# The second block's keys, receptances and values as seven half-size products, in a stage of their own behind the gates' plain tile

## The chip, the cores and the metric

The kernel runs on one core of a Trainium2 chip. The metric is the device time of one execution in microseconds (us); lower is better. One core has a matrix engine (TensorE, PE in the rows), a vector engine (VectorE, DVE), a scalar engine (ScalarE, ACT), GpSimd (POOL) and a sync engine (SyncE, SP) that issues the weight transfers. Each runs its own instruction list in order; semaphores make one wait for another.

## The reference

Three transformer blocks run one after the other on 512 tokens of width 1024, in float32. The change is in the second block, where 16 meta tokens come in front (528 tokens). What matters of it:

```python
def centred_shift(p, mu):
    prev = jnp.pad(p[:, :-1], ((0, 0), (1, 0), (0, 0)))
    nxt = jnp.pad(p[:, 1:], ((0, 0), (0, 1), (0, 0)))
    return p + mu[0] * (prev - p) + mu[1] * (nxt - p)
...
    u = rms_norm(h, mix_norm_g[i])
    proj = u @ w_in[i]
    p_rwkv, p_q, p_k, p_v, p_gate_a, p_gate_b = jnp.split(proj, IN_SPLITS, axis=-1)
...
    z = centred_shift(p, shift_mu)
    r, k, v, wd, ad, gd = jnp.split(z, RWKV_SPLITS, axis=-1)
```

So the first 1952 columns of the projection, 512 each for receptances (r), keys (k) and values (v) and 416 for the low-rank inputs of decay, in-context rate and gate, are products of the normed activations, and each is then mixed with its neighbours in time: own part times (1 - mu0 - mu1), plus mu0 times the token before, plus mu1 times the token behind. The keys are also scaled by `k_k` and normed per head of 64. From these a two-directional recurrence over the 528 tokens starts.

## The kernel before

**Layout.** Activations stand with channels on the 128 partitions and the 528 tokens along the free dimension, in slabs of eight 128-channel chunks. `H` is the normed input, `X` the residual, `S2` to `S6` work slabs. Weights come in tiles of 1024 x 512 through a ring of slots (SyncE, `issue_weights`).

**The stage (lines 2365 to 2369).** One `DenseStage` computes four weight tiles: `rwkv_gates` (chunks 12 to 15, the last of 32 channels), `rwkv_k` (4 to 7), `rwkv_r` (0 to 3), `rwkv_v` (8 to 11). Its unit is one chunk by one half of the tokens (264): eight accumulating matmuls (line 393), then a ScalarE copy out of PSUM into `raw` (`keep_raw`, line 2287). After the second half of a chunk VectorE mixes it (`shift`): own part (2282), token before (2283), token behind (2285). There are 32 units; four PSUM banks go round.

**What sets the order.** Each engine's list is written out by `woven`: after every unit each *lane* may put one step of side work. Lane one, from unit 1: `FirstNorm` (827), the norm of the first block's end, eight steps on VectorE. Lane two, from unit 10: `Gates` (on ScalarE a tanh and two sigmoids at 2248 to 2250, then eight small products 2241 and 2242 with a ScalarE copy 2255 each), then `unit_keys`, a `HeadNorm` of the keys (squares 923 on ScalarE, sums 888 and 896 on TensorE, root on ScalarE, floor and reciprocal 955 and 959 on VectorE, then four times a spread 911 on TensorE and a scaling 964 on VectorE). Lane three, from unit 16: `Factors` of the recurrence's first piece (products 3104 and 3114 on TensorE, ScalarE 3120 to 3155, VectorE 3182 to 3231). Ahead of the first unit stand the block's norms (`TwoNorms`).

**Stage ends.** A stage is a block: all engines meet at its end before any begins the next. After this one comes `recurrence` (first matmuls at line 3344).

**Seven products.** `SevenProducts` (2516) exists already and is used by other matrices here. It takes two chunks (a pair) and both token halves as a 2 x 2 block product and needs seven products of four matmuls where plain units need 32 matmuls. Per pair, VectorE makes sums of weights ("third", "second", "first", "fourth", each 128x512, lines 2714, 2746, 2749, 2767) and puts the seven banks together with seven 128x264 additions (2758 to 2778); ScalarE copies two banks (2688, 2692). Products go in the order 4, 1, 6, 7, 2, 5, 3: product 6 waits for "second", product 3 for "fourth". A lane step stands behind product 1, 7, 5 and 3: four steps per pair. In a `SevenStage` VectorE's lanes are one step behind those of the other engines (`later`). `post` is what is done with a finished pair; with `by="dve"` VectorE does it in the next pair's first step, behind that pair's "second" and "first", or, at the end of a matrix, before anything of the next matrix (`finish`). Before, no pair of the recurrence's inputs goes this way.

## Time and profile before

| | us |
|---|---|
| median of 3 runs | 3779.97 (3779.03 to 3781.15) |
| span of the profiled execution | 3776.2 |
| TensorE busy | 3490.8 (92% of the span) |
| VectorE busy | 1319.4 (35%) |
| ScalarE busy | 665.2 (18%) |
| first unit of the stage to the first matmul of the recurrence | 1659.63 to 1807.46 |

The profiled span is 3.8 us below the median of the runs; what lies around the span is not in the profile. Times in the rows count from the span's start. A timeline row gives a group of like instructions: start, time to the end of the last, engine, line, what it writes and reads, and in brackets the idle time before it and who ended it. One matmul on float32 shows as two records, so "x16" there is eight matmuls.

### The profile page before, as it was taken

The numbers are of one execution on the slowest core, as the hardware profiler recorded it, in microseconds if no ns is written. First come the engines' busy times: TensorE is split into PE (matmuls) and PEld (weight loads), VectorE is DVE, ScalarE is ACT, GpSimd is POOL, SyncE is SP. The second block draws the span as 40 slices with busy tenths as digits, with TensorE's granted clock in tenths as the row PEclk, the third lists the DMA queues.
The fourth block names the chain that finished last, engine by engine and source line by source line (L and its number), as shares of the span: only waits on it lengthen the run. The fifth ranks groups of instructions, "written<-read, shape, count | busy, mean of one in ns | idle before, by whom it ended". The sixth has DMA issues, their size and how long they took to land. (4 is left out here: it accounts for less than half of the span.)

```text
span 3776.2 us, 56173 instructions
## 1 busy us (share of the span) xinstructions
PE 3490.8 (92%) x24676; PEld 2304.4 (61%) x24676; DVE 1319.4 (35%) x2796; ACT 665.2 (18%) x1461; POOL 78.3 (2%) x128
## 2 busy tenths in 40 slices
PE   8999999798988889889888899999999999999997
PEld 4444678433332333257667777778888855887666
DVE  1211456310111101133666344345533623544344
ACT  2111540200000000013343114112100001101231
POOL 0000000000000000000222000000000000000000
PEclk9999999999999999999999899999999999999999
DMA  6233101799999999950000210222222111221110
GB/s 252 103 132 112 45 24 49 315 428 427 428 428 425 423 427 427 426 214 1 3 4 4 85 56 23 79 82 88 68 90 90 67 67 54 81 89 34 53 62 23
DMA packets 125842, 593.73 MB, mean 157 GB/s; under 512 B 7296, under 2 KB 37632, under 8 KB 99232
## 3 DMA queue, kind: packets, MB, share of 16 engines
q1 hardware_dynamic: 125600, 590.14, 39.2%
q8 instruction: 196, 3.21, 0.4%
q14 instruction: 46, 0.38, 0.0%
HBM read 588.02 MB, written 2.10 MB: 156 GB/s over the span
## 5 line engine op out<-in xcount | busy, mean ns | idle before, releaser
L2656 PE MATMUL banks<-slabs,ring 128*128 128x256 f32 (+1 forms) x3472 | 770.4, 382 | 0.2 <-DVE ring L2767 0.2
L2656 PEld LDWEIGHTS banks<-slabs,ring 128*128 128x128 f32 x3472 | 657.3, 190 | 103.6 <-issue 7.6
L1991 PE MATMUL banks<-ring,slabs 128*64 128x512 f32 x2304 | 520.2, 599 | 80.6 <-DMA ring<-in_w_exp 69.3
L393 PE MATMUL banks<-slabs,ring 128*128 128x264 f32 (+3 forms) x1736 | 568.5, 485 | 6.0 <-PEq L323 2.5
L393 PEld LDWEIGHTS banks<-slabs,ring 128*128 128x128 f32 (+1 forms) x1736 | 326.9, 191 | 222.2 <-issue 186.6
L1991 PEld LDWEIGHTS banks<-ring,slabs 128*64 128x64 f32 x2304 | 163.4, 137 | 413.1 <-issue 318.7
L2128 DVE TENSOR_TENSOR work<-work,banks 128x512 f32<-128x512 f32 x32 | 22.0, 687 | 487.3 <-PE banks L1991 487.3
L1991 PE MATMUL banks<-slabs 128*64 128x512 f32 x768 | 171.9, 596 | 21.4 <-DMA slabs<-in_w_exp 18.5
L2861 PE MATMUL banks<-slabs,ring 128*128 128x264 f32 x768 | 172.4, 386 | 1.6 <-issue 1.6
L2861 PEld LDWEIGHTS banks<-slabs,ring 128*128 128x128 f32 x768 | 145.8, 190 | 26.8 <-issue 1.9
L393 PE MATMUL banks<-ring,slabs 128*128 128x512 f32 (+3 forms) x560 | 158.6, 439 | 0.8 <-PEq L323 0.8
L2636 PE MATMUL banks<-slabs,ring 128*128 128x256 f32 (+1 forms) x576 | 135.4, 395 | 9.4 <-PEq L323 7.5
L1991 PEld LDWEIGHTS banks<-slabs 128*64 128x64 f32 x768 | 54.4, 137 | 132.2 <-issue 107.6
L393 PEld LDWEIGHTS banks<-ring,slabs 128*128 128x128 f32 (+1 forms) x560 | 91.2, 188 | 70.3 <-issue 67.5
L2636 PEld LDWEIGHTS banks<-slabs,ring 128*128 128x128 f32 x576 | 111.4, 196 | 32.1 <-issue 13.1
L2072 ACT ACTIVATE work<-banks 128x512 f32<-128x512 f32 x32 | 19.1, 597 | 542.7 <-PE banks L1991 542.7
L2135 DVE COPY slabs<-banks 64x512 f32<-64x512 f32 x32 | 22.0, 689 | 261.2 <-PE banks L1991 261.0
L1297 ACT ACTIVATE slabs<-slabs,small 128x513 f32<-128x513 f32 (+7 forms) x136 | 97.1, 714 | 88.3 <-DVE small L1253 88.2
L2746 DVE TENSOR_TENSOR ring<-ring 128x512 f32<-128x512 f32 (+1 forms) x65 | 46.6, 717 | 174.9 <-PE banks L2656 171.6
L1168 PE MATMUL banks<-slabs 64*128 64x256 f32 (+10 forms) x544 | 97.3, 438 | 8.8 <-DVE small L1249 4.5
L2688 ACT COPY slabs<-banks 128x256 f32<-128x256 f32 (+1 forms) x51 | 19.2, 376 | 402.0 <-PE banks L2656 402.0
L2656 PE MATMUL banks<-ring 128*128 128x256 f32 (+1 forms) x336 | 78.8, 384 | 0.0
(544 smaller groups left out, 3841.7 us busy)
## 6 DMA issues: line engine op xcount, KB each, us to landing
ring<-in_w_exp SPq DMA_DIRECT2D x144, 2048.0 KB, 15.8
slabs<-in_w_exp SPq DMA_DIRECT2D x48, 2048.0 KB, 31.8
ring<-in_w_in SPq DMA_DIRECT2D x19, 2048.0 KB, 10.9
ring<-in_w_ff SPq DMA_DIRECT2D x16, 2048.0 KB, 8.2
ring<-in_even_w_in SPq DMA_DIRECT2D x14, 2048.0 KB, 8.0
ring<-in_w_ada SPq DMA_DIRECT2D x12, 2048.0 KB, 8.1
ring<-in_w_out SPq DMA_DIRECT2D x4, 2048.0 KB, 8.2
ring<-in_even_w_out SPq DMA_DIRECT2D x4, 2048.0 KB, 7.8
```

The source lines that it names most:

```text
L393: mm = core.nc.tensor.matmul(to, lhsT, rhs, start=kk0 + k < g, stop=kk0 + k >= kcs - g)
L1168: mm = nc.tensor.matmul(score[h][0:m, at:at + cols], *products[j], start=j == 0, stop=j == count - 1)
L1297: nc.scalar.activation(r, r, ACT.Exp, bias=st[0:m, h:h + 1], scale=scale, accum_out=st[0:m, 2 + h:3 + h]).then_inc(e_ready.sem, e_ready.ad ...
L1991: ins = mm(out[64 * c:64 * c + CAP, :], lhsT[:, k, :], w[:, at:at + 512], start=first and k == 0, stop=last and k == 3)
L2072: nc.scalar.activation(sg, G[:, :], ACT.Silu).then_inc(moe["silu"].sem, moe["silu"].add(1))
L2128: nc.vector.tensor_tensor(hid, sg, U[:, :], ALU.mult).then_inc(moe["hidden"].sem, moe["hidden"].add(1))
L2135: ins = nc.vector.tensor_copy(y[64 * s:64 * s + CAP, 512 * half:512 * half + 512], Y[64 * half:64 * half + CAP, :])
L2636: last = mm(self.bank["plain", at], A[i][k // h][:, k % h, :], self.B[k // h][j][:, k % h, :], start=k == 0, stop=k == 2 * h - 1)
L2656: last = mm(self.bank[p, which], a[:, k, :], b[:, k, :], start=k == 0, stop=k == h - 1)
L2688: self.done(nc.scalar.copy(self.to(p, 1, 0), self.bank[p, 4]), "held")
L2746: self.done(tt(A[1][1], A[1][1], A[1][0], ALU.subtract), "second")
L2861: last = mm(self.bank(which), a[:, k, :], self.fourth(t, k) if which == 4 else b[:, k, :], start=t == 0 and k == 0, stop=t == 1 and k == 7)
```

## The change

The stage is cut in two. A `DenseStage` keeps the gates' tile alone, with `FirstNorm` beside it and a new side, `HalfSums`, which makes the four sums of `H` (128x1056 each) into `S3`. A `SevenStage` behind it computes keys, receptances and values as two pairs each by `SevenProducts`, without a plain first pair, all three on the same sums and the same small scratch; `Gates` and `unit_keys` run in its lane from step 0, `Factors` from step 10 of 24. The mixing's own part becomes a ScalarE activation with a scale per partition (`own_part`, two of 128x528 per pair), done before the next pair's first copy; the two neighbour parts stay on VectorE (`neighbours`, four instructions per pair) as `post`. A pair's second set of two scratch buffers goes. Semaphores are shared out anew so that the stage has the counts it needs.

```diff
--- before
+++ after
-    raw, z = [S2, S3], [S4, S5]
+    raw, z, four = S2, [S4, S5], 4
...
-        p_, z_ = raw[ch // KC][rows, ch % KC, :], z[ch // KC][rows, ch % KC, :]
+        p_, z_ = raw[rows, ch % KC, :], z[ch // KC][rows, ch % KC, :]
         step(nc.vector.tensor_scalar(z_, p_, own[rows, ch:ch + 1], None, ALU.mult))
...
-    keep_raw = lambda eng, ps, ch, t0, t1: nc.scalar.copy(raw[ch // KC][0:ps.shape[0], ch % KC, t0:t1], ps)
+    keep_raw = lambda eng, ps, ch, t0, t1: nc.scalar.copy(raw[0:ps.shape[0], ch % KC, t0:t1], ps)
+    raw_of = lambda at, p: raw[:, at + 2 * p:at + 2 * p + 2, :]
+
+    def own_part(at, first):
+
+        def scaled(act, p):
+            for i in range(2):
+                ch = first + 2 * p + i
+                ins = nc.scalar.activation(z[ch // KC][:, ch % KC, :], raw_of(at, p)[:, i, :], ACT.Copy, scale=own[:, ch:ch + 1])
+            return ins
+        return scaled
+
+    def neighbours(at, first):
+
+        def post(dve, p):
+            step = Chain(dve, shifted)
+            for i in range(2):
+                ch = first + 2 * p + i
+                p_, z_ = raw_of(at, p)[:, i, :], z[ch // KC][:, ch % KC, :]
+                step(nc.vector.scalar_tensor_tensor(out=z_[:, 1:T], in0=p_[:, 0:T - 1], scalar=core.col("mu0", ch), in1=z_[:, 1:T], op0=ALU.mult, op1=ALU.add))
+                ins = nc.vector.scalar_tensor_tensor(out=z_[:, 0:T - 1], in0=p_[:, 1:T], scalar=core.col("mu1", ch), in1=z_[:, 0:T - 1],
+                                                     op0=ALU.mult, op1=ALU.add)
+            return ins
+        return post
...
-    def gates_shifted(act):
-
-        act.wait_ge(shifted.sem, shifted.at(3 * 4))
-    gates = Gates(core, 1, S5, gw, g, T, gates_shifted)
-    gates_pe = gates.pe
-
-    def after_loads(pe):
-
-        pe.wait_ge(core.loaded.sem, core.loaded.at(16 * len(loads)))
-        yield from gates_pe(pe)
-    gates.pe = after_loads
+    gates = Gates(core, 1, S5, gw, g, T, lambda act: None)
     first = FirstNorm(norms, lambda k: core.col("final", k))
     unit_keys = HeadNorm(core, 2, S4[:, 4:8], 4, T, S6[:, 4:8], core.rstd[:, :], core.c("common", "halves32"), core.c("common", "pick8"), 2, 1, 0.0,
                          lambda c: gains[:, 16 + c:17 + c], S6[:, 4:8], (6, 5, 6), core.work[:, 2 * RW + 2 * WIDE:2 * RW + 2 * WIDE + 50],
-                         first=lambda act, c: act.wait_ge(shifted.sem, shifted.at(3 * (5 + c))), scale=lambda c: core.col("k_k", c), floor=1e-12)
...
     def after_gates(pe):
 
         pe.wait_ge(gates.s["chunk"].sem, gates.s["chunk"].at(8))
-        pe.wait_ge(first.s["shifted"].sem, first.s["shifted"].at(1))
         yield from keys_pe(pe)
     unit_keys.pe = after_gates
+
+    in_halves = lambda k, a, b: H[:, 4 * k:4 * k + 4, a:b]
+    def products(name, at, first, places):
+        return SevenProducts(core, name, in_halves, T, core.slab[3], places, lambda p: raw_of(at, p), neighbours(at, first), "dve", plain=False,
+                             sums_of=name, scaled=own_part(at, first))
+    places = spare[:, :, :].rearrange("p k c -> p (k c)")[:, 4 * WIDE:]
+    some = lambda: Carve(places)
+    keys, receptances, values = products("rwkv_k", 0, 4, some()), products("rwkv_r", 4, 0, some()), products("rwkv_v", 0, 8, some())
+    values.place_free = lambda engine, p: keys.pair_done(engine, p)
+    sums_of_h = HalfSums(keys, core.rwkv["step"], lambda dve: dve.wait_ge(norms.s["chunk"].sem, norms.s["chunk"].at(KC)))
...
         if what == "keys":
-            chunk(8)
+            keys.pair_done(engine, 0)
+            receptances.pair_done(engine, 0)
         if what == "unit_keys":
...
-            chunk(12)
+            values.pair_done(engine, 0)
...
-    DenseStage(core, [("rwkv_gates", units_of(of_h, T, keep_raw, post=("dve", shift), first=12)),
-                      ("rwkv_k", units_of(of_h, T, keep_raw, post=("dve", shift), first=4)),
-                      ("rwkv_r", units_of(of_h, T, keep_raw, post=("dve", shift))),
-                      ("rwkv_v", units_of(of_h, T, keep_raw, post=("dve", shift), first=8))],
-               banks=range(4), before=[norms], loads=loads, lanes=[(1, [first]), (10, [gates, unit_keys]), (16, [ahead_of_tiles])], pool_too=True).run()
+    DenseStage(core, [("rwkv_gates", units_of(of_h, T, keep_raw, post=("dve", shift), first=12))], banks=range(4), before=[norms], loads=loads,
+               lanes=[(1, [first]), (3, [sums_of_h])]).run()
+    SevenStage(core, [keys, receptances, values], banks=range(4), lanes=[(0, [gates, unit_keys]), (10, [ahead_of_tiles])], pool_too=True).run()
...
         else:
             self.after(engine, "out12", p - self.plain + 1)
+        if self.scaled:
+            self.after(engine, "scaled", p - self.plain + 1)
         self.done(self.post(engine, p), "rows")
...
             nth = p - self.plain + 1
+            if self.scaled and nth > 1:
+                self.after(act, "out12", nth - 1)
+                self.done(self.scaled(act, p - 1), "scaled")
             self.product_done(act, p, 4)
             self.place_free(act, p)
...
+        if self.scaled:
+            self.after(act, "out12", self.count - self.plain)
+            self.done(self.scaled(act, self.count - 1), "scaled")
...
-            s1, u2, u3 = self.s1[p % 2], self.u2[p % 2], self.u3[p % 2]
+            s1, u2, u3 = self.s1[p % 2], self.u2, self.u3
...
+class HalfSums(Side):
+
+
+    def __init__(self, products, count, ready):
+        self.products, self.count, self.inputs_ready = products, count, ready
+
+    def pe(self, pe):
+        yield
+
+    act = pe
+
+    def dve(self, dve):
+        tt, step = self.products.core.nc.vector.tensor_tensor, Chain(dve, self.count)
+        B, (T1, T2, T3, T4) = self.products.B, self.products.T
+        self.inputs_ready(dve)
+        tt(T3, B[1][1], B[0][1], ALU.subtract)
+        step(tt(T1, B[0][1], B[0][0], ALU.subtract))
+        yield
+        step(tt(T2, B[1][1], T1, ALU.subtract))
+        yield
+        tt(T4, B[1][0], T2, ALU.subtract)
+        yield
```

Line numbers of the changed kernel differ: matmuls of the seven products stand at 2653, gates' products at 2240 and 2241, unit keys' at 887, 895 and 910, `Factors`' at 3173 and 3183; on VectorE the neighbour parts at 2305 and 2306, "third", "second", "first" at 2759, 2791, 2794, the last addition of a pair at 2823, `HeadNorm` at 954, 958 and 963, `Factors` from 3251 to 3300.

The first place is VectorE's list around the reciprocals of the unit keys. Before, from the mixing of one chunk on:

```order
L2282 TENSOR_SCALAR slabs<-slabs,small 128x528
L2283 SCALAR_TENSOR_TENSOR slabs<-slabs,param 128x527
L2285 SCALAR_TENSOR_TENSOR slabs<-slabs,param 128x527
L955 TENSOR_SCALAR work<-work 128x32
L955 TENSOR_SCALAR work<-work 16x8
L959 RECIPROCAL work<-work 128x32
L959 RECIPROCAL work<-work 16x8
L964 SCALAR_TENSOR_TENSOR slabs<-slabs,gains,banks 128x528
```

Now, from "second" of the second pair of receptances on:

```order
L2791 TENSOR_TENSOR ring<-ring 128x4x128
L2794 TENSOR_TENSOR ring<-ring 128x4x128
L2305 SCALAR_TENSOR_TENSOR slabs<-slabs,param 128x527
L2306 SCALAR_TENSOR_TENSOR slabs<-slabs,param 128x527
L2305 SCALAR_TENSOR_TENSOR slabs<-slabs,param 128x527
L2306 SCALAR_TENSOR_TENSOR slabs<-slabs,param 128x527
L954 TENSOR_SCALAR work<-work 128x32
L954 TENSOR_SCALAR work<-work 16x8
L958 RECIPROCAL work<-work 128x32
L958 RECIPROCAL work<-work 16x8
L963 SCALAR_TENSOR_TENSOR slabs<-slabs,gains,banks 128x528
```

Between the mixing's three instructions and the reciprocals (955, 959) there was nothing else; now "second", "first" (which needs the pair's product 1) and the four neighbour parts of the pair before stand ahead of them (954, 958).

The second place is TensorE's list there. Before:

```order
L393 MATMUL banks<-slabs,ring 128x264 x8
L3104 MATMUL banks<-slabs,work 128x264
L393 MATMUL banks<-slabs,ring 128x264 x8
L911 MATMUL banks<-common,work 64x128 x8
L911 MATMUL banks<-common,work 64x16 x2
L3104 MATMUL banks<-slabs,work 128x264
```

Now:

```order
L2653 MATMUL banks<-slabs,ring 128x264 x4
L3173 MATMUL banks<-slabs,work 128x264
L2653 MATMUL banks<-slabs,ring 128x264 x8
L910 MATMUL banks<-common,work 64x128 x8
L910 MATMUL banks<-common,work 64x16 x2
L3173 MATMUL banks<-slabs,work 128x264
```

The spread of the first chunk (911 before, 910 now), which reads the reciprocals, stands behind the pair's products 4 and 1, and products 6 and 7 behind it.

The third place is the end of VectorE's list in the stage. Before:

```order
L3222 TENSOR_TENSOR slabs<-slabs 128x528
L3223 SCALAR_TENSOR_TENSOR slabs<-slabs,param 128x528
L2282 TENSOR_SCALAR slabs<-slabs,small 128x528
L2283 SCALAR_TENSOR_TENSOR slabs<-slabs,param 128x527
L2285 SCALAR_TENSOR_TENSOR slabs<-slabs,param 128x527
L3231 SCALAR_TENSOR_TENSOR slabs<-banks,ring 128x264 x2
L2282 TENSOR_SCALAR slabs<-slabs,small 128x528
L2283 SCALAR_TENSOR_TENSOR slabs<-slabs,param 128x527
L2285 SCALAR_TENSOR_TENSOR slabs<-slabs,param 128x527
```

Now:

```order
L2816 TENSOR_TENSOR slabs<-banks,ring 128x264
L3288 TENSOR_TENSOR ring<-ring,slabs 128x2x528
L3289 TENSOR_TENSOR ring<-ring,work 128x2x528
L2823 TENSOR_TENSOR slabs<-banks,ring 128x264
L3291 TENSOR_TENSOR slabs<-slabs 128x528
L3292 SCALAR_TENSOR_TENSOR slabs<-slabs,param 128x528
L2305 SCALAR_TENSOR_TENSOR slabs<-slabs,param 128x527
L2306 SCALAR_TENSOR_TENSOR slabs<-slabs,param 128x527
L2305 SCALAR_TENSOR_TENSOR slabs<-slabs,param 128x527
L2306 SCALAR_TENSOR_TENSOR slabs<-slabs,param 128x527
L3300 SCALAR_TENSOR_TENSOR slabs<-banks,ring 128x264 x2
```

The last chunk's mixing, three instructions, was the end, with the recurrence's bonus (3231) ahead of it; now two chunks' neighbour parts stand behind the last addition (2823) and two of `Factors`, and the bonus (3300) behind them.

## Rows read from the trace of the kernel before

**Rows 1.** The page: span, and TensorE busy over it (share, instructions).

```profile
span 3776.2 us, 56173 instructions
...
PE 3490.8 (92%) x24676; PEld 2304.4 (61%) x24676; DVE 1319.4 (35%) x2796; ACT 665.2 (18%) x1461; POOL 78.3 (2%) x128
```

**Rows 2.** Windows of 20 us: busy (count) by engine; PEclk; DMA share, GB/s.

```profile
1680.00:1700.00 20.00, 20.00 (x90) 14.09 (x89) 9.05 (x13) 1.87 (x5) 0.00 (x0) 1.00 0.30 105
...
1780.00:1800.00 20.00, 20.00 (x106) 16.79 (x105) 15.47 (x20) 4.48 (x8) 0.00 (x0) 1.00 0.00 1
```

**Rows 3.** Timeline of TensorE: start, us, line, [idle before <-releaser].

```profile
1656.06 3.78 PE L764 MATMUL banks<-common,small 128*128 128x128 f32 x16
...
1659.63 44.33 PE L393 MATMUL banks<-slabs,ring 128*128 128x264 f32 x192
...
1705.31 0.71 PE L2241 MATMUL banks<-slabs,ring 128*128 128x264 f32 x2 [1.34 <-ACT slabs L2250]
...
1706.59 3.83 PE L393 MATMUL banks<-slabs,ring 128*128 128x264 f32 x16
...
1747.40 2.88 PE L888 MATMUL banks<-slabs,common 128*32 128x512 f32 x16 [1.19 <-ACT slabs L923]
...
1764.33 1.31 PE L911 MATMUL banks<-common,work 128*64 128x128 f32 x20
...
1807.46 1.16 PE L3344 MATMUL banks<-ring 64*64 64x64 f32 x64 [3.09 <-PEq L323]
```

**Rows 4.** Groups by line and shape, 1650 to 1810: count, busy, mean ns, idle before.

```profile
L2283 DVE SCALAR_TENSOR_TENSOR slabs<-slabs,param 128x527 f32<-128x527 f32 x15 | 11.5, 768 | 0.5
...
L2282 DVE TENSOR_SCALAR slabs<-slabs,small 128x528 f32<-128x528 f32 x15 | 7.3, 488 | 57.5 <-ACT slabs L2287 57.5
```

**Rows 5.** Timeline of VectorE, same columns, in and after the stage.

```profile
1691.28 0.75 DVE L2285 SCALAR_TENSOR_TENSOR slabs<-slabs,param 32x527 f32<-32x527 f32 x1
...
1762.66 0.24 DVE L955 TENSOR_SCALAR work<-work 128x32 f32<-128x32 f32 x2
...
1762.93 0.40 DVE L959 RECIPROCAL work<-work 128x32 f32<-128x32 f32 x2
...
1787.53 1.26 DVE L3216 TENSOR_TENSOR ring<-ring,slabs 128x1056 f32<-128x1056 f32 x1
...
1800.92 0.43 DVE L3231 SCALAR_TENSOR_TENSOR slabs<-banks,ring 128x264 f32<-128x264 f32 x1 [1.55 <-PE banks L3114]
...
1806.15 0.77 DVE L2285 SCALAR_TENSOR_TENSOR slabs<-slabs,param 128x527 f32<-128x527 f32 x1
```

**Rows 6.** Timeline of ScalarE: four 128x528 activations.

```profile
1746.52 2.61 ACT L923 ACTIVATE slabs<-slabs,param 128x528 f32<-128x528 f32 x4
```

**Rows 7.** Timeline of TensorE in the seven-product stage of wo2, and its end.

```profile
2459.27 37.54 PE L2656 MATMUL banks<-slabs,ring 128*128 128x264 f32 x168
...
2499.99 2.04 PE L572 MATMUL banks<-slabs,common 128*32 128x512 f32 x32 [3.17 <-PEq L323]
```

**Rows 8.** Timeline of VectorE in that stage, one pair of chunks.

```profile
2475.49 0.69 DVE L2749 TENSOR_TENSOR ring<-ring 128x512 f32<-128x512 f32 x1 [1.09 <-PE banks L2656]
...
2479.05 0.43 DVE L2761 TENSOR_TENSOR slabs<-banks,slabs 128x264 f32<-128x264 f32 x1 [1.35 <-PE banks L2656]
```

**Rows 9.** Windows of 1 us: TensorE busy and PEclk, its granted clock.

```profile
712.00:713.00 1.00, 1.00 (x7) 1.00 (x7) 0.00 (x0) 0.00 (x0) 0.00 (x0) 0.59 1.04 442
...
1654.00:1655.00 1.00, 0.46 (x5) 0.38 (x4) 0.56 (x4) 0.24 (x2) 0.00 (x0) 0.95 0.00 0
...
1661.00:1662.00 1.00, 1.00 (x4) 0.82 (x3) 1.00 (x3) 0.00 (x0) 0.00 (x0) 0.64 0.00 0
...
1808.00:1809.00 1.00, 1.00 (x44) 0.93 (x37) 0.30 (x2) 0.70 (x1) 1.00 (x2) 0.75 0.00 0
...
2500.00:2501.00 1.00, 1.00 (x20) 0.45 (x24) 0.00 (x0) 0.00 (x0) 0.00 (x0) 1.00 1.04 375
```

**Rows 10.** Timeline of TensorE after a long idle time in the first block.

```profile
709.62 5.35 PE L1960 MATMUL banks<-area,slabs 128*128 128x128 f32 x32 [1.56 <-DVE area L2110]
```

64 lines of the change are left out of this document (40 added, 24 removed).

## The prediction

> **What bounds the kernel now.** I read first the page's busy shares, then windows of 20 us over the stage, then the three engines' timelines in it. The page gives TensorE 92% of the 3776.2 us span [rows 1]; in the stage it is 20.00 of 20 us busy in nearly every window, at clock 1.00, while VectorE is at 9.05 where only mixing runs and at 15.47 in the last full window, where `Factors` has joined in [rows 2]. So TensorE bounds the stage, with two small stalls of 1.34 us (the gates' product waiting for tanh and sigmoid) and 1.19 us (unit keys' sums waiting for squares) [rows 3]. Behind the last unit TensorE is idle 3.09 us until the recurrence's first matmul at 1807.46 [rows 3]: the last chunk is still mixed, the last instruction starting at 1806.15 and lasting 0.77 [rows 5], so the next stage starts 0.54 us after VectorE's end. The reader is to see two things: what is saved on TensorE counts in full, as long as TensorE stays the bound; and the stage's end is set by VectorE.
>
> **What TensorE saves.** 192 records take 44.33 us and two records are one matmul, so a matmul of 264 columns is 0.46 us with the slow start, and less without: the wo2 stage, seven products at the same size, does 84 in 37.54 us without a pause, 0.445 each [rows 3, 7]. Keys, receptances and values were 24 units of 8, 192 matmuls. Now they are six pairs of 28, 168 matmuls. 24 x 0.445 = **10.7 us saved**. The wait of 1.19 us goes too, since the gates' and keys' work lies differently: squares are ready before the sums are reached. The gates' wait for tanh and sigmoid, 1.34 us, stays, since their chain still starts behind the second copy and TensorE has as much to do as before until the first small product; I take +0.2. The lanes' TensorE work is the same, but the two bonus products, with their switching 1.2 us, move behind the stage's last product and are counted there. Sum: -10.7 - 1.2 + 0.2 - 1.2 = **-12.9 us**.
>
> **The new stage border.** The 192 records are 12 units in 44.33 us, so the gates' eight units end 29.6 us behind 1659.63, near 1689.4 with the last drain [rows 3]. VectorE still mixes that chunk of 32 channels, its last part ending at 1692.03 [rows 5], and then has two steps of `FirstNorm` left, 0.75 each (this kind of instruction takes 0.768 on 527 columns, and these are 512 [rows 4]), to 1693.5. All engines meet, 0.54 us as at the recurrence's start. TensorE starts again at 1694.0: **+4.6 us** in which before it had work. `HalfSums` (four of 128x1056 at 1.26 [rows 5]) lies under the units of the gates, in which VectorE has over half its time free; I cost it at nothing.
>
> **The work on VectorE.** Own parts go: 12 x 0.488 = 5.9 us [rows 4]. Weight sums and additions come: per pair four at 0.69 and seven at 0.43 [rows 8], 5.8 us, for six pairs 35. That is cheap where VectorE waits anyway; where it does not, its order decides. I walked the three lists step by step with the rows' durations: 0.80 us from an instruction to one that depends on it and 0.68 to one that does not for the neighbour parts (so a pair's four take 3.0), and 0.20 from a product's end to its reader. TensorE's stalls in that walk:
>
> - Keys to receptances. The last keys pair is put together 0.65 after its last product; ScalarE (behind a gates' copy) makes the own parts, 2 x 0.65 [rows 6]; VectorE mixes, 3.0, and only then makes "third" and "second" of the receptances, 1.4. TensorE meanwhile has products 4 and 1 and two gates' products, 6.1 us, and waits **1.1**.
> - The unit keys' reciprocals. Before, floor and reciprocal ran at 1762.66, and the spread at 1764.33 found them done [rows 3, 5]. Now they stand behind "first", which needs product 1 of the same pair, and behind four neighbour parts; TensorE meets the spread right after product 1. That is 0.2 + 0.6 + 3.0 + 0.7 (955 and 959 together [rows 5]), less the little that overlaps: **4.4**.
> - Receptances to values: like the first, with a `HeadNorm` scaling and a scan of 1.36 before it, **1.8**.
> - The last pair. From "first" on VectorE never pauses: 0.6, mixing 3.0, two of `Factors` 1.4, three additions 1.3, a 128x1056 and a 128x528 of `Factors` 2.0; only then "fourth", 0.7, for which product 3 waits: **2.0**.
>
> Together **+9.3 us**, no row of which the trace of before shows. Then the end: behind product 3 stand VectorE's two 128x1056 (2.3, partly under it), the last addition, two of `Factors` 1.5 (ScalarE's own parts lie under them), the last two chunks' mixing 3.0, a bonus 0.43, the second bonus product, which TensorE may only start when the first bank is read (one matmul 0.45 and two handovers, 0.8), a bonus 0.43 [rows 5], and 0.54 to the next stage. From product 3's end to the recurrence I get 8.4 us, before it was 3.3: **+5.1 us**.
>
> Sum at full clock: -12.9 + 4.6 + 9.3 + 5.1 = **+6.1 us**. The part of it that is a sum of rows in a fixed order (border, end) I hold to within 1 us; the four stalls hang on the walk, 9.3 with an error of 3 either way.
>
> **The clock.** Rows show TensorE's granted clock at either 1.00 or 0.50, which is 2.4 and 1.2 GHz. Behind the 3.09 us of idleness and small 64-column work at 1807.46 it fell (0.75 is the mean of the microsecond in which it did); at 2500, after an idle 3.17 us, it was still 1.00 [rows 3, 7, 9]. The new border (4.6 us) and the wait for the reciprocals (4.4) are longer than any gap in this stage, so no row decides whether dense work behind them starts slow. When it was low and dense work came, it rose late: 709.62 to about 712.8 and, with a low start at 1656.06, about 1661.7 [rows 3, 9, 10], that is 3.2 to 5.7 us at half rate. It costs half of that, 1.6 to 2.8 us; I take 2.2 for each of the two gaps, and 0.6 for the recurrence's first matmuls (1.16 us), which so far began at full clock. The bounds are 0 and 6.2. I take the low clock at both, since the idle time is half as long again as the one at 2500 that just held. Together **+5.0 us**. On this the Trainium skill ("TensorE: Matmul & The Clock Gate", section "Why this matters for your kernels") has a rule that speaks against the change: no idle gaps between bursts of matmuls in mid kernel, since idleness brings the half clock back. By it both gaps pay and the sum stays at +11; by the row at 2500 alone neither pays and it is +6.
>
> The Trainium skill ("Perfetto Trace Analysis", section "Optimizing Scalar/DVE Operations") also says that moving work to ScalarE pays where VectorE is saturated. In the windows here VectorE is not saturated before [rows 2]; at the new end it is, but there the moved part is hidden on ScalarE, and the order, not the load, makes the wait.
>
> **Forecast.** +6.1 + 5.0 = +11.1 us on the profiled execution's 3776.2, which stands 3.8 below the median. On the median that is 3780.0 + 11.1 = **3791.1 us**.
>
> **Rivals.**
> - *The clock holds.* Same stalls, no low clock: +6.1, **3786.1**. For it speaks 2500, against it the length of the gaps.
> - *The order is kinder than I walked it: not slower.* If ScalarE and VectorE finish each pair early enough that TensorE never waits at the four places, only border and end remain: -12.9 + 4.6 + 5.1 = -3.2, **3776.8**, and with the stalls half as long 3781. It decides at the reciprocals: if they are done within products 6 and 7's time. VectorE's load over the stage is only some 75 us of 119 (35 of sums and additions, 24 x 0.768 = 18 of neighbour parts [rows 4], some 20 of `Factors` and unit keys), which speaks for it; the lists as they now stand speak against it.
> - *VectorE falls further behind.* The end is a chain of some 19 us on one engine; if each dependent step costs 0.1 us more than the rows (scratch in one buffer, not two), or ScalarE's own parts come behind `Factors`' activations, stalls grow by 5 and the clock falls once more: +17, **3797**.
> - *The own part does not leave the path.* ScalarE's two activations stand between the last addition and the mixing, 1.3 us plus two handovers, where before VectorE took 1.0. Where nothing hides it (both changes of matrix) it adds 0.7 each; that is in the 1.1 and 1.8 already and no case of its own.
>
> **Chances.** Forecast with low clock at one or both gaps 0.60 (3787.5 to 3794), clock holds 0.17, kinder order 0.12, further behind 0.11. The range takes the forecast, the clock's rival and half of each outer one (0.6 + 0.17 + 0.11): 3782 to 3797, the bounds of the walk's error on either side of it. Over 0.2%, 7.6 us, is about what a measurement of this kernel can tell from no change: slower, from 3787.5 up, is 0.58 of the forecast's case, 0.04 of the clock's and 0.10 of the last, together 0.72; same is 0.25; faster, below 3772.4, needs the kinder order and some gain that I have no term for, 0.03.
>
> **What would show it.** In the changed profile: 24 fewer matmuls in the stage; TensorE idle about 4.6 us between the gates' tile and the first product; a wait of about 4.4 us of the first spread of the unit keys (910) for the reciprocals (958); waits of 1 to 2 us of products for "second" at receptances' and values' first pairs and for "fourth" in the last; 8 us from the last product to the recurrence's first matmul, only bonus products in it; and half clock for 3 to 6 us behind the first two. I am wrong if the spread finds its reciprocals ready, if the clock stays at 1.00, or if time moves in the recurrence, which has the same instructions as before.

## The result and the profile after

| | before | after |
|---|---|---|
| device time, median of 4 runs | 3779.5 us (3778.5 to 3781.2) | 3793.8 us (3792.9 to 3796.0) |
| profiled execution's span | 3776.2 us | 3792.3 us |
| mean granted TensorE clock | 0.982 | 0.977 |
| gates' first unit to the recurrence's first matmul | 147.83 us | 161.70 us |
| of it, TensorE busy | 142.21 us | 141.24 us |
| of it, TensorE idle | 5.62 us | 20.46 us |
| mean granted clock in it | 0.99 | 0.90 |

After over before is 1.0038, with a 95% interval of 1.0024 to 1.0053: slower, by 14 us. The page of the changed kernel, beside [rows 1]:

```profile
span 3792.3 us, 56192 instructions
...
PE 3492.1 (92%) x24628; PEld 2306.6 (61%) x24628; DVE 1350.1 (36%) x2854; ACT 669.3 (18%) x1461; POOL 77.7 (2%) x128
```

The stretch that the change touches is measured from the gates' first unit to the recurrence's first matmul [rows 3]; I call it the stretch from here on. Its whole-window row in the changed kernel (busy time and count of PE, PEld, DVE, ACT, POOL; granted clock; DMA share; GB/s):

```profile
1659.49:1821.19 161.70, 141.24 (x623) 104.69 (x623) 91.13 (x152) 39.06 (x71) 0.40 (x4) 0.90 0.04 14
```

It is 13.9 us longer than before, of the 16.1 by which the two profiles differ. The recurrence behind it is as long as it was: 304.20 us from its first matmul to the next stage's, before 304.32. The rest of the kernel, span less stretch, is 3628.4 us before and 3630.6 after, and in the runs below it scatters between 3623 and 3632 without a cause in the code. So here the stretch is the ruler, and the device time only confirms its sign. The stretch has a scatter of its own, since each kernel has one profile: the first four products behind the border took 9.04, 9.89, 10.06 and 10.41 us in four kernels whose lists are the same up to there. I therefore read a difference between two stretches row by row, and take one of under 3 us, my estimate from such rows, as no difference by itself.

TensorE's timeline in the changed kernel (start, us, engine and line, operands, count, [idle before it <- what ended the idle]). L392 is the gates' plain tile, L2653 the seven products, L910 the unit keys' spread, L3183 the two bonus products, L3413 the recurrence. This answers to [rows 3]:

```profile
1659.49 29.90 PE L392 MATMUL banks<-slabs,ring 128*128 128x264 f32 x128
1693.65 9.89 PE L2653 MATMUL banks<-slabs,ring 128*128 128x264 f32 x32 [4.26 <-PEq L322]
1704.87 0.71 PE L2240 MATMUL banks<-slabs,ring 128*128 128x264 f32 x2 [1.34 <-ACT slabs L2249]
...
1738.07 3.80 PE L2653 MATMUL banks<-slabs,ring 128*128 128x264 f32 x16 [1.53 <-DVE ring L2791]
1741.80 1.11 PE L887 MATMUL banks<-slabs,common 128*32 128x512 f32 x16
...
1758.95 2.30 PE L910 MATMUL banks<-common,work 128*64 128x128 f32 x20 [4.34 <-DVE work L958]
1761.19 1.25 PE L3173 MATMUL banks<-slabs,work 64*128 64x264 f32 x2
1762.36 6.12 PE L2653 MATMUL banks<-slabs,ring 128*128 128x264 f32 x16
...
1786.35 5.49 PE L2653 MATMUL banks<-slabs,ring 128*128 128x264 f32 x16 [2.10 <-DVE ring L2791]
...
1810.63 3.10 PE L2653 MATMUL banks<-slabs,ring 128*128 128x264 f32 x8 [1.94 <-DVE ring L2812]
1815.68 1.25 PE L3183 MATMUL banks<-slabs,common 128*128 128x264 f32 x2 [1.95 <-DVE slabs L3292]
1819.15 1.25 PE L3183 MATMUL banks<-slabs,common 128*128 128x264 f32 x2 [2.23 <-DVE slabs L3300]
1821.19 1.99 PE L3413 MATMUL banks<-ring 64*64 64x64 f32 x64 [0.79 <-PEq L322]
```

VectorE's rows at the two longest of these waits: the last steps of `FirstNorm` (L826) ahead of the border, and "first" (L2794), the last of the four neighbour parts (L2306) and the reciprocals (L958) ahead of the spread:

```profile
1691.92 1.41 DVE L826 SCALAR_TENSOR_TENSOR slabs<-slabs,param,banks 128x512 f32<-128x512 f32 x2
...
1754.65 0.69 DVE L2794 TENSOR_TENSOR ring<-ring 128x512 f32<-128x512 f32 x1 [1.03 <-PE banks L2653]
...
1757.54 0.77 DVE L2306 SCALAR_TENSOR_TENSOR slabs<-slabs,param 128x527 f32<-128x527 f32 x1
...
1758.50 0.40 DVE L958 RECIPROCAL work<-work 128x32 f32<-128x32 f32 x2
```

The times in brackets in TensorE's timeline add up to the 20.5 us of idleness: 4.26 at the border, 1.34 for tanh and sigmoid, 1.53 and 2.10 for "second" (L2791) at the receptances' and the values' first pairs, 4.34 for the reciprocals (L958), 1.94 for "fourth" (L2812) and 1.95, 2.23 and 0.79 at the end. Before they were three rows, 1.34, 1.19 and 3.09 [rows 3]. So 14.8 us of idle time came. And the busy time hardly fell, though 24 matmuls are gone. The groups by line show why (count; busy us, mean ns; idle before):

```profile
L2653 PE MATMUL banks<-slabs,ring 128*128 128x264 f32 x336 | 87.3, 418 | 9.8 <-PEq L322 4.3 <-DVE ring L2791 3.6 <-DVE ring L2812 1.9
L392 PE MATMUL banks<-slabs,ring 128*128 128x264 f32 (+1 forms) x128 | 29.9, 395 | 0.0
```

L392 and L2653 together take 117.2 us; before, the 512 records of the same kind took 119.9 in this stretch. The 418 ns of L2653 against 395 of L392 are its slow parts: the group of 32 at 1693.65 takes 9.89 us, where the same group takes 7.36 at full clock (in a run below), and a group of 16 takes 3.83 at full clock, but 6.12 at 1762.36 and 5.49 at 1786.35. One-microsecond windows of the changed kernel behind the border, in the wait for the reciprocals, behind the wait of 2.10 us, and in product 3 of the last pair; before, the windows of the stretch that [rows 2] shows read 1.00:

```profile
1692.00:1693.00 1.00, 0.00 (x0) 0.00 (x0) 1.00 (x2) 0.00 (x0) 0.00 (x0) 0.50 1.06 412
1757.00:1758.00 1.00, 0.00 (x0) 0.00 (x0) 0.96 (x2) 0.00 (x0) 0.00 (x0) 0.50 0.00 0
1788.00:1789.00 1.00, 1.00 (x4) 0.80 (x3) 0.00 (x0) 0.00 (x0) 0.00 (x0) 0.50 0.00 0
1812.00:1813.00 1.00, 1.00 (x3) 0.77 (x3) 1.00 (x2) 0.00 (x0) 0.00 (x0) 0.50 0.00 0
```

The low clock's cost from the rows:

| where | at low clock | at full clock | lost |
|---|---|---|---|
| first four products | 9.89 | 7.36 | 2.5 |
| spread, a lane's product, group of 16 behind it | 2.30 + 1.25 + 6.12 | 1.31 + 0.71 + 3.83 | 3.8 |
| group of 16 behind the 2.10 us | 5.49 | 3.83 | 1.7 |
| product 3 of the last pair | 3.10 | 2.05 | 1.0, hidden under VectorE |
| the two bonus products | 2 x 1.25 | 2 x 0.71 | 1.1, the first hidden |

That is 10.1 us of busy time, of which some 8.5 lengthen the stretch. It eats up most of the 10.2 us of busy time that the 24 matmuls had given (119.9 less 109.7, which is 117.2 at full clock).

### The profile page after: what moved, and what is told of

It reads as the page before. It is cut to its first block and busy times, and to the rows that moved or that the text cites. A ratio compares the mean times of both kernels' runs of the same rounds, so it can differ in the third digit from the quotient of the medians.

```text
span 3792.3 us, 56192 instructions
## 1 busy us (share of the span) xinstructions
PE 3492.1 (92%) x24628; PEld 2306.6 (61%) x24628; DVE 1350.1 (36%) x2854; ACT 669.3 (18%) x1461; POOL 77.7 (2%) x128
## 5 line engine op out<-in xcount | busy, mean ns | idle before, releaser
L2653 PE MATMUL banks<-slabs,ring 128*128 128x256 f32 (+1 forms) x3808 | 857.7, 385 | 10.1 <-PEq L322 4.3
L2653 PEld LDWEIGHTS banks<-slabs,ring 128*128 128x128 f32 x3808 | 724.6, 191 | 132.1 <-issue 24.2
L392 PE MATMUL banks<-slabs,ring 128*128 128x512 f32 (+3 forms) x1352 | 477.5, 511 | 6.0 <-PEq L322 2.5
L392 PEld LDWEIGHTS banks<-slabs,ring 128*128 128x128 f32 (+1 forms) x1352 | 254.6, 191 | 205.4 <-issue 181.4
L2930 PEld LDWEIGHTS banks<-slabs,ring 128*128 128x128 f32 x768 | 145.8, 190 | 26.8 <-issue 1.9
L392 PE MATMUL banks<-ring,slabs 128*128 128x512 f32 (+3 forms) x560 | 158.6, 439 | 0.8 <-PEq L322 0.8
L2674 PE MATMUL banks<-slabs,ring 128*128 128x256 f32 (+1 forms) x576 | 135.9, 398 | 9.4 <-PEq L322 7.5
L392 PEld LDWEIGHTS banks<-ring,slabs 128*128 128x128 f32 (+1 forms) x560 | 91.2, 188 | 70.3 <-issue 67.5
L2674 PEld LDWEIGHTS banks<-slabs,ring 128*128 128x128 f32 x576 | 113.6, 199 | 30.4 <-issue 12.8
L2791 DVE TENSOR_TENSOR ring<-ring 128x512 f32<-128x512 f32 (+1 forms) x71 | 50.8, 715 | 183.8 <-PE banks L2653 178.9
L2730 ACT COPY slabs<-banks 128x264 f32<-128x264 f32 (+1 forms) x57 | 21.5, 377 | 410.7 <-PE banks L2653 410.7
L2653 PE MATMUL banks<-ring 128*128 128x256 f32 (+1 forms) x336 | 78.7, 384 | 0.0
## 6 DMA issues: line engine op xcount, KB each, us to landing
ring<-in_w_in SPq DMA_DIRECT2D x19, 2048.0 KB, 11.1
```

The lines of the kernel that those rows point to most:

```text
L392: mm = core.nc.tensor.matmul(to, lhsT, rhs, start=kk0 + k < g, stop=kk0 + k >= kcs - g)
L2653: last = mm(bank, a[:, k, :], b[:, k, :], start=k == 0, stop=k == h - 1)
L2674: last = mm(self.bank["plain", at], A[i][k // h][:, k % h, :], self.B[k // h][j][:, k % h, :], start=k == 0, stop=k == 2 * h - 1)
L2730: self.done(nc.scalar.copy(self.to(p, 1, 0), self.bank[p, 4]), "held")
L2791: self.done(tt(A[1][1], A[1][1], A[1][0], ALU.subtract), "second")
L2930: last = mm(self.bank(which), a[:, k, :], self.fourth(t, k) if which == 4 else b[:, k, :], start=t == 0 and k == 0, stop=t == 1 and k == 7)
```

## The experiments

Each kernel is a small edit away from a neighbour. The four of the first group ran on one chip beside the kernel before (median 3777.5 us there), the next three on one with it at 3779.9, the last with it at 3778.7. Ratios are to the kernel before of the same group.

| kernel | stretch | time, ratio [95%] |
|---|---|---|
| before | 147.8 | 1 |
| after | 161.7 | 1.0038 [1.0024, 1.0053] |
| the border alone (e1_split_plain) | 153.8 | 1.0019 [1.0009, 1.0028] |
| after, reciprocals sooner (e2_lane_before_mixing) | 154.3 | 1.0017 [1.0007, 1.0026] |
| after, fillers in two waits (e3_filler) | 155.5 | 1.0026 [1.0017, 1.0035] |
| after, own part on VectorE (e4_own_on_vector) | 166.1 | 1.0039 [1.0025, 1.0054] |
| after, one stage (e5_one_stage) | 147.4 | 0.9990 [0.9981, 0.9999] |
| e5 and two orders (e6_one_stage_orders) | 145.5 | 0.9994 [0.9985, 1.0003] |
| after and the two orders (e7_two_stages_orders) | 151.3 | 0.9999 [0.9990, 1.0008] |
| e6, later idle turn out, end reordered (e8_end_order) | 142.9 | 0.9982 [0.9973, 0.9991] |

**The border alone.** The kernel before with its stage cut in two behind the gates; keys, receptances and values stay plain units, mixing as before.

```diff
-    DenseStage(core, [("rwkv_gates", units_of(of_h, T, keep_raw, post=("dve", shift), first=12)),
-                      ("rwkv_k", units_of(of_h, T, keep_raw, post=("dve", shift), first=4)),
...
+    DenseStage(core, [("rwkv_gates", units_of(of_h, T, keep_raw, post=("dve", shift), first=12))], banks=range(4), before=[norms], loads=loads, lanes=[(1, [first])]).run()
+    DenseStage(core, [("rwkv_k", units_of(of_h, T, keep_raw, post=("dve", shift), first=4)),
...
-               banks=range(4), before=[norms], loads=loads, lanes=[(1, [first]), (10, [gates, unit_keys]), (16, [ahead_of_tiles])], pool_too=True).run()
+               banks=range(4), lanes=[(2, [gates, unit_keys]), (8, [ahead_of_tiles])], pool_too=True).run()
```

> The kernel before with its stage cut in two and nothing else: the gates' tile with FirstNorm in one stage, keys, receptances and values as 24 plain units in the next, Gates and unit keys from its unit 2, Factors from its unit 8 (places they had before). It prices the new border by itself. My theory (a border is idle time plus a low clock behind it): TensorE idle about 4.3 us behind the gates' tile, half clock for 3 to 5 us behind that, so the recurrence's first matmul 6 to 7 us later than before and the time 3785 to 3787. Rival (the border is only the idle time; what the changed kernel lost beyond it is the seven products' own): 4.3 us, 3783 to 3784, clock at 1.00.

TensorE's timeline, the border and the end:

```profile
1692.16 16.16 PE L393 MATMUL banks<-slabs,ring 128*128 128x264 f32 x64 [4.26 <-PEq L323]
...
1811.82 1.98 PE L3335 MATMUL banks<-ring 64*64 64x64 f32 x64 [3.09 <-PEq L323]
```

The stretch is 153.82 us, 6.0 longer: 4.26 idle, the same figure as in the changed kernel, and 1.7 of low clock in the group behind it (16.16 us, where 64 such records take 14.51 at full clock). The end's 3.09 is that of before. A border costs 6 to 7 us here, whether plain units follow it (4.26 + 1.7) or seven products (4.26 + 2.5). This kernel has no `HalfSums`, and its border is no shorter: the sums of `H` cost nothing, as forecast.

**The reciprocals sooner.** VectorE takes its turn for the unit keys ahead of the four neighbour parts of the pair before, not behind them. Nothing else changes.

```diff
-            if self.post and self.by == "dve" and p:
+            if self.post and self.by == "dve" and p and not self.scaled:
                 self.finish(dve, p - 1)
...
             yield
+            if self.post and self.by == "dve" and p and self.scaled:
+                self.finish(dve, p - 1)
```

> The changed kernel with one edit: a pair's neighbour parts come behind VectorE's lane step of the next pair's first step, not ahead of it, so the unit keys' floor and reciprocal stand right behind first. My theory (the 4.34 us wait for the reciprocals is the four neighbour parts ahead of them, and the 3.8 us of half-clock work behind it is that wait's doing): the wait falls to 1.3 to 1.6 us, the clock stays at 1.00 there, the time falls by 5 to 7 us to 3787 to 3789. Rival (it is VectorE's load, not its order: what is moved comes back behind): the wait goes to product 3 or the next second, the time stays within 2 us of the changed kernel's 3793.8.

```profile
1738.12 3.80 PE L2653 MATMUL banks<-slabs,ring 128*128 128x264 f32 x16 [1.53 <-DVE ring L2791]
...
1756.04 1.31 PE L910 MATMUL banks<-common,work 128*64 128x128 f32 x20 [1.38 <-DVE work L958]
...
1779.62 5.49 PE L2653 MATMUL banks<-slabs,ring 128*128 128x264 f32 x16 [2.10 <-DVE ring L2791]
...
1803.90 3.27 PE L2653 MATMUL banks<-slabs,ring 128*128 128x264 f32 x8 [1.94 <-DVE ring L2814]
```

The spread now waits 1.38 us and runs in 1.31, at full clock; the stretch is 154.26 us, 7.4 shorter. By the rows, 3.0 of this is the wait (1.38 for 4.34) and 3.8 the low clock behind it. Another 0.9 is a shorter low clock behind the border (9.04 for 9.89), which the edit doesn't reach, and the end is 0.2 longer. The products' waits are the changed kernel's to the hundredth (1.53, 2.10, 1.94), and the group behind the 2.10 again takes 5.49, so the rival, by which the wait comes back further on, is refuted. The reciprocals' place thus cost 6.8 us: of the wait of 4.34, forecast as 4.4, the neighbour parts were 3.0, and the clock was 3.8 against the 2.2 of the prediction.

**Fillers.** The changed kernel with 8 and 9 matmuls whose result nobody reads, put where TensorE would wait at the border and for the reciprocals. VectorE's and ScalarE's lists stay as they are, so only the clock can gain.

```diff
-                lanes=[(1, [first]), (3, [sums_of_h])]).run()
+                lanes=[(1, [first]), (3, [sums_of_h]), (7, [Filler(core, H, core.bank[4], 8)])]).run()
...
+    unit_keys.filler = Filler(core, H, core.bank[5], 9)
```

> The changed kernel with matmuls that nobody reads in its two longest idle places: 8 of 264 columns (3.6 us) behind the gates' last unit, 9 (4.0 us) ahead of the wait for the reciprocals. No wait is taken away. My theory (of the 13.7 us that the stage grew, half is work at half clock): the idle time proper falls to under 1 us at both, products behind them run at full clock, and 2.7 + 3.8 = 6.5 us come back, time 3786 to 3788. Rival (the clock costs little, the waits are the loss): less than 2 us come back, or it gets slower since the filler delays the spread.

```profile
1693.34 7.36 PE L2657 MATMUL banks<-slabs,ring 128*128 128x264 f32 x32 [0.51 <-PEq L322]
...
1735.23 5.49 PE L2657 MATMUL banks<-slabs,ring 128*128 128x264 f32 x16 [1.53 <-DVE ring L2795]
...
1757.80 1.31 PE L913 MATMUL banks<-common,work 128*64 128x128 f32 x20 [0.33 <-DVE work L961]
...
1781.37 3.80 PE L2657 MATMUL banks<-slabs,ring 128*128 128x264 f32 x16 [2.09 <-DVE ring L2795]
```

Both covered places run at full clock: 7.36 us for the group of 32, 1.31 for the spread. The stretch is 155.52, shorter by 6.2 (6.5 expected), though useless work was added; the same products take 7.36 in place of 9.89 us. That shows that the low clock is a cost of its own beside the idleness. What I had not expected stands in the other two rows: now the clock fell behind the wait of 1.53 us (5.49 for 16), which it had outlasted in the changed kernel, and outlasted the 2.09. Whether the fillers did this isn't shown: the next kernel has a fall that no edit explains.

**The own part on VectorE.** The seven products stay; ScalarE's own part goes back to VectorE as in the kernel before.

```diff
+                step(nc.vector.tensor_scalar(z_, p_, own[:, ch:ch + 1], None, ALU.mult))
...
-                             sums_of=name, scaled=own_part(at, first))
+                             sums_of=name)
```

> The changed kernel with the mixing's own part back on VectorE: six instructions of neighbour and own parts per pair in place of four, ScalarE's two activations gone. It tells what the ScalarE part does. My theory (it matters only where VectorE's order is the path): a pair's mixing takes 4.0 in place of 3.0 us; at the two changes of matrix ScalarE's hop of 2.8 us goes and the wait for second becomes 0.5 to 1.5 us shorter; the wait for the reciprocals grows to 5.3 and the end by 1.0 us; the sum is 0 to 2 us slower, 3794 to 3796. Rival (the part's move to ScalarE is what makes the hop and so the loss): 2 us or more faster.

```profile
1739.06 3.80 PE L2654 MATMUL banks<-slabs,ring 128*128 128x264 f32 x16 [0.24 <-DVE ring L2792]
...
1760.99 2.30 PE L910 MATMUL banks<-common,work 128*64 128x128 f32 x20 [5.39 <-DVE work L958]
...
1788.60 5.48 PE L2654 MATMUL banks<-slabs,ring 128*128 128x264 f32 x16 [2.74 <-DVE ring L2792]
...
1813.93 2.02 PE L2654 MATMUL banks<-slabs,ring 128*128 128x264 f32 x8 [3.00 <-DVE ring L2813]
...
1823.32 1.25 PE L3184 MATMUL banks<-slabs,common 128*128 128x264 f32 x2 [3.50 <-DVE slabs L3301]
```

The stretch is 166.07 us, 4.4 longer, but 2.5 of it lie ahead of the first instruction that the edit touches. The gates' tile takes 30.19 for 29.90 us, the four products behind the border 10.41 for 9.89, and the group of 16 behind the wait for tanh and sigmoid, 1.34 us in both kernels, 5.49 for 3.83:

```profile
1706.77 5.49 PE L2654 MATMUL banks<-slabs,ring 128*128 128x264 f32 x16
```

There the clock fell in a place where the two kernels' lists are the same, so it isn't the edit's doing. Some 1.9 us are left for the edit. The wait at keys to receptances nearly vanished (0.24 for 1.53: VectorE is quicker than the detour over ScalarE where nothing is queued), the later ones grew, by 0.6 to 1.3 us each: 5.39 for the reciprocals, 2.74 at the values, 3.00 ahead of product 3, 3.00 and 3.50 ahead of the two bonus products (in the changed kernel 4.34, 2.10, 1.94, 1.95, 2.23). Together the waits are 3.8 us longer; product 3 and the first bonus, here at or near full clock, give part of it back. In device time the two kernels can't be told apart (1.0039 and 1.0038). The loss of the change isn't in ScalarE's own part, which by the waits is worth its place.

**One stage.** The changed kernel with the gates' tile as the first part of the seven-product stage. The border is gone; the lanes' turns are counted through, which also moves them.

```diff
+    plain = PlainTile(core, "rwkv_gates", of_h, T, keep_raw, shift, 12)
+    SevenStage(core, [plain, keys, receptances, values], banks=range(4), before=[norms], loads=loads,
+               lanes=[(1, [first]), (3, [sums_of_h]), (10, [gates, unit_keys]), (18, [ahead_of_tiles])], pool_too=True).run()
```

> The changed kernel without the border between the two stages: the gates' plain tile is a part of the same stage as the seven products, so TensorE goes from the gates' last unit to the first product without waiting for all engines; VectorE's order is that of the changed kernel. My theory: the wait of 4.26 us ahead of the first product goes, and with it the low clock of the first four products (9.89 against 7.2, 2.7 us); the wait behind the reciprocals (4.3 us and its low clock) and the waits at the changes of matrix (1.5 and 2.1) stay. Sum: the stretch from the gates' first unit to the recurrence's first matmul goes from 161.7 us to about 155, the time to about 3787 (6 to 8 us under the changed kernel). Rival: VectorE's chain to the end is the bound and TensorE only gets there sooner: then the waits at the changes of matrix and ahead of the eighth lane grow by what the border gives back, the stretch stays at 159 to 162 and the time at 3792 to 3795.

```profile
1693.39 9.14 PE L2667 MATMUL banks<-slabs,ring 128*128 128x264 f32 x40 [1.07 <-DVE ring L2805]
...
1727.56 5.49 PE L2667 MATMUL banks<-slabs,ring 128*128 128x264 f32 x16 [1.53 <-DVE ring L2805]
...
1759.34 1.31 PE L910 MATMUL banks<-common,work 128*64 128x128 f32 x20 [1.45 <-DVE work L958]
...
1771.64 3.80 PE L2667 MATMUL banks<-slabs,ring 128*128 128x264 f32 x16 [0.85 <-DVE ring L2805]
...
1806.01 1.99 PE L3481 MATMUL banks<-ring 64*64 64x64 f32 x64 [0.79 <-PEq L322]
```

The stretch is 147.35 us: 14.3 shorter, twice what I expected. The border's 6.8 us (4.26 and 2.5) went as said. The other half I had missed: with the turns counted through, the unit keys' step on VectorE falls into a turn that has no neighbour parts ahead of it (1758.61, behind an addition), and TensorE meets the spread four products later, behind 27 and not 23; so the wait is 1.45 and keeps its clock. The merge did what the second experiment's order does. The wait of 1.53 stands again, here with low clock behind it, and there is a new one of 1.07 in the keys' first pair, whose "second" now stands behind the gates' mixing. Other rows moved too: the wait of 1.34 us for tanh and sigmoid is gone, the one at the values is 0.85 and keeps its clock (2.9 us less), and the unit keys' sums run in 2.26 us where they took 1.11.

**Both orders, in one stage and in two.** The neighbour parts behind the lane's turn as above, and the last pair's additions and neighbours at a change of matrix done within the next matrix's first pair. Both kernels also have an idle turn ahead of the unit keys' step.

```diff
+            if self.owed and p == self.plain:
+                self.owed.finish(dve, self.owed.count - 1)
...
-        if self.post and self.by == "dve":
+        if self.post and self.by == "dve" and not self.owes:
             self.finish(dve, self.count - 1)
```

> The kernel of the previous run with two orders more: the second block's mixing neighbours behind the unit keys' step, so that the reciprocals come sooner, and at a change of matrix the last pair's additions owed to the next matrix's first pair. My theory: all stalls but those of the last pair are then gone: of 161.7 us the border's 7, the reciprocals' 7.4, and the changes of matrix 1.5 + 2.1 + 1.7 of low clock, or 142 to 145 us against the 147.8 of the kernel before; time 3774 to 3778, 2 to 6 us faster than before. Rival: the additions owed are late in the next matrix and reach the eighth lane and the end: then the end's 7.8 us grows by 3 to 6 and the stretch is 148 to 150, the time that of before.

> The changed kernel with its two stages and the same two orders as the previous run. My theory: the reciprocals' 7.4 and the changes' 5.3 go and the border's 7 stays: 149 to 151 us, time 3780 to 3783, 1 to 3 us over before. Rival: the clock, which is low until the fourth product behind the border, falls again at the first wait that is left (as with the fillers): 1.7 to 3.8 us of this come back, 152 to 154 us, time 3783 to 3786.

The one-stage kernel, TensorE:

```profile
1694.35 9.14 PE L2669 MATMUL banks<-slabs,ring 128*128 128x264 f32 x40 [1.07 <-DVE ring L2807]
...
1744.88 2.88 PE L887 MATMUL banks<-slabs,common 128*32 128x512 f32 x16 [1.19 <-ACT slabs L922]
...
1761.26 1.31 PE L910 MATMUL banks<-common,work 128*64 128x128 f32 x20 [1.17 <-DVE work L958]
...
1794.10 3.52 PE L2669 MATMUL banks<-slabs,ring 128*128 128x264 f32 x8 [1.94 <-DVE ring L2832]
```

The two-stage kernel:

```profile
1693.26 10.06 PE L2655 MATMUL banks<-slabs,ring 128*128 128x264 f32 x32 [4.27 <-PEq L322]
...
1758.61 1.31 PE L910 MATMUL banks<-common,work 128*64 128x128 f32 x20 [1.58 <-DVE work L958]
...
1760.76 5.20 PE L2655 MATMUL banks<-slabs,ring 128*128 128x264 f32 x16
```

Neither waits for "second" at the receptances' or the values' first pair any more. Stretches: 145.45 us in one stage and 151.34 in two. The border is the largest part of the difference of 5.9 (4.27 idle and 2.7 in the first group), less the 1.07 us that the one-stage kernel waits in the keys' first pair and 3.0 us that it loses at the squares; the two-stage kernel has 1.34 and a fall of the clock more. The one-stage kernel is just above the 142 to 145 us that I expected; the idle turn ahead of the unit keys moved ScalarE's squares back, so that their sums wait 1.19 us and then run at the squares' pace (2.88 for 1.11). The two-stage kernel is just above its 149 to 151: the clock falls behind a wait of 1.58 us (5.20 for 16), as the rival said, but costs 1.6 us there and the stretch stays under the rival's 152.

**The end.** The one-stage kernel with both orders, without the idle turn, and with VectorE's last four neighbour parts moved into the time between the two bonus products.

```diff
-               lanes=[(1, [first]), (3, [sums_of_h]), (10, [gates, Idle(1), unit_keys]), (18, [ahead_of_tiles])], pool_too=True).run()
+               lanes=[(1, [first]), (3, [sums_of_h]), (10, [gates, unit_keys]), (18, [ahead_of_tiles])], pool_too=True).run()
...
+        if self.turn_more:
+            yield
         if self.post and self.by == "dve" and not self.owes:
```

> The kernel with one stage and two orders, with two orders changed: no idle turn ahead of the unit keys' step, so that ScalarE's squares (there 1743.99, 0.9 us before TensorE's sums want them) start a turn sooner, and VectorE's last neighbours of the values a turn later, in the 1.34 us in which it waits for the second bonus product. My theory: the sums' wait of 1.19 us and their slow run (2.88 against 1.11) go, and 1 to 1.5 us of the end; of 145.45 us 141 to 143 are left, time 3772 to 3776, faster than before by 0.1 to 0.2%. Rival: the recurrence's first input needs the last neighbours, or the wait ahead of the reciprocals grows by the turn taken out: 144 to 146 us and the time of the run it comes from (3775 to 3778).

```profile
1740.65 2.26 PE L887 MATMUL banks<-slabs,common 128*32 128x512 f32 x16
...
1758.48 1.31 PE L910 MATMUL banks<-common,work 128*64 128x128 f32 x20 [1.45 <-DVE work L958]
...
1793.72 2.02 PE L2669 MATMUL banks<-slabs,ring 128*128 128x264 f32 x8 [1.94 <-DVE ring L2832]
1798.75 0.71 PE L3259 MATMUL banks<-slabs,common 128*128 128x264 f32 x2 [3.01 <-DVE slabs L3368]
1800.07 1.25 PE L3259 MATMUL banks<-slabs,common 128*128 128x264 f32 x2 [0.60 <-DVE slabs L3376]
1803.63 1.98 PE L3489 MATMUL banks<-ring 64*64 64x64 f32 x64 [2.32 <-PEq L322]
```

142.94 us, as expected, and 0.9982 [0.9973, 0.9991] of the time before: this one is faster than both kernels, 3771.8 us where the kernel before has 3778.7 in the same group. The two edits are not told apart by a run, but the rows part them: the sums' wait is gone, though they take 2.26 us and not the 1.11 I had expected, and from the start of product 3 to the recurrence it is 9.9 us for 11.0, of which some 0.4 is that product 3 ran at full clock here (2.02 us for 3.52). The busy time of TensorE in the stretch is 132.55 us, idle time 10.39. Of the idle time 7.9 stands ahead of the last product and behind it (1.94 + 3.01 + 0.60 + 2.32): VectorE's chain to the end, which is left as the bound.

## Why the prediction came out

It was right in sign and size: 3793.8 us measured for 3791.1, within 3782 to 3797. That range is 15 us wide and has room for the clock's rival too; what speaks for the mechanism is that the waits forecast came, each at its place and near its length. By its own steps:

- **TensorE's saving.** 24 matmuls at 0.445, 10.7 us: the groups of 264 columns with weights from the ring give 119.9 before, and 117.2 less 7.5 of low clock (2.5 + 2.3 + 1.7 + 1.0) after, 10.2. Right. The wait for tanh and sigmoid stayed at 1.34 us, where I had added 0.2. At the unit keys' sums I counted only the wait of 1.19 us. The sums themselves had run at the pace of the squares, 2.88 us [rows 3]; with the squares ready they take 1.11. That is 1.8 more of gain than my term.
- **The border.** +4.6 forecast, 4.26 of idle time in the changed kernel and in the kernel with the border alone. Right.
- **The four stalls.** +9.3 forecast as 1.1, 4.4, 1.8 and 2.0; the waits are 1.53, 4.34, 2.10 and 1.94, together 9.9. Walking VectorE's list instruction by instruction gave each to within 0.4 us.
- **The end.** +5.1 forecast (8.4 for 3.3). From the last product's end, taken at full clock since VectorE hides the rest, 1812.7 to 1821.19 less 0.5 of a slow bonus product, 8.0; before, the rows have 3.1, not 3.3 [rows 3]. So +4.9. Right, though no run changes this term alone.
- **Sum at full clock.** +6.1 forecast. Measured 13.9 less 8.5 of low clock, +5.4. The single terms give 0.7 less than that (-10.2 - 3.0 - 1.2 + 4.3 + 9.9 + 4.9 = +4.7). Such a sum counts the ends of groups that the next group overlaps: the group of 16 at 1706.15 in the changed kernel lasts 3.83 us, and the next begins 3.67 us behind its start. That may be the 0.7; I have not shown it.
- **The clock.** Here the step failed in size. I gave 2.2 us to each of two gaps and 0.6 to the recurrence, 5.0. Measured are 2.5 at the border, 3.8 behind the reciprocals, 1.7 at a third place that I had not named, the values' first pair, and 0.5 at the bonus, 8.5. The 2.2 rested on 3.2 to 5.7 us of work at half clock; behind the reciprocals the low clock lasted from the spread's start at 1758.95 to about 1767.0, 8 us. Nothing was lost at the recurrence, whose slow first group (1.99 for 1.16) left its length as it was. The third fall came behind a wait of 2.10 us, and I had given waits of that size no low clock, since 3.17 us had held at 2500 [rows 7, 9].

So the clock was 3.5 us too small and the gain at the unit keys' sums 1.8 too small, errors of opposite sign that partly cancel, which was luck; and the two profiles' other 2.2 us lie outside the stretch, within the scatter that the rest of the kernel shows from run to run.

**The rule on gaps.** The clock fell behind the border and the reciprocals, as the rule would have it that I set beside the row at 2500 (the Trainium skill, "TensorE: Matmul & The Clock Gate", section "Why this matters for your kernels", which asks for no long idle gap between bursts of matmuls in mid kernel). Behind the two gaps of over 4 us the trace agrees. The rule goes by the length of the gap, and here the length alone did not decide, so the measurement stands against it: a gap of 3.17 us held [rows 7, 9], and gaps of 2.10 and, in one run, 1.34 us had a fall behind them.

**The rivals.** That the clock holds is refuted by the changed kernel itself and by the fillers. The kinder order did not come by itself, but it is a matter of order alone: with "second" and the reciprocals ahead of the neighbour parts the waits for "second" go and that for the reciprocals falls to 1.2 to 1.6 us, as the runs with both orders show. The change then pays in one stage (0.9982, with the end reordered too); with the border it comes out even (0.9999). Further behind, with stalls 5 us longer, is near what the own part on VectorE made of it, 3.8 us of waits; its price of +17 was added up wrongly, since 11.1 + 5 + one more fall at 2.2 is 18.3. One part of this rival came in the changed kernel: the clock did fall once more. That ScalarE's own part stays on the path was true only at keys to receptances, 1.3 us (1.53 against 0.24) for the 0.7 I gave.

Of the 13.9 us, the border was 6.8 (4.26 idle and 2.5 of low clock) and the reciprocals' place 6.8 (3.0 and 3.8); without these two the stretch would be 148.1. The run in one stage, in which both are gone, has 147.35, but single rows moved in it both ways, so that the nearness is in part chance. What then remains, 3.6 us of waits for "second" with 1.7 of low clock, 1.9 for "fourth", 1.4 for the reciprocals and an end that is 4.9 longer with 0.5 of low clock, about uses up what the products and the squares save. The orders of the later runs take the first two of these away too; in one stage, with the end reordered, the time falls below that of the kernel before.

## What to carry to other kernels

A saving on a saturated engine counts only while it stays saturated: list, for each place where it now depends on another engine, what stands ahead in that engine's queue, and put what is waited for ahead of what nobody waits for yet. Here two lines of order were worth 6.8 us, more than half of what the products save, and took no work away. A stage border costs the last engine's tail and then the slow start behind it, about 6 to 7 us here, so a cheaper form of work that needs a stage of its own has to earn that first. Price each wait of TensorE twice, as idle time and as half clock behind it; fillers or another order tell the two apart.
